# The token gather of a mixture-of-experts group, cut into four parts that each feed their own step of the gate product

## What is computed

```python
def ec_moe(h, w_r, w_gate, w_up, w_down):
    bsz, n, _ = h.shape
    cap = max(1, EC_CAPACITY * n // N_EXPERTS)          # 32 tokens per expert
    aff = jax.nn.softmax(jnp.einsum("bnd,de->bne", h, w_r).astype(jnp.float32), axis=-1)
    gates, idx = lax.top_k(jnp.swapaxes(aff, 1, 2), cap)
    bidx = jnp.broadcast_to(jnp.arange(bsz)[:, None, None], idx.shape)
    xs = h[bidx, idx]
    hid = jax.nn.silu(jnp.einsum("becd,edf->becf", xs, w_gate)) * jnp.einsum("becd,edf->becf", xs, w_up)
    ys = jnp.einsum("becf,efd->becd", hid, w_down) * gates[..., None].astype(h.dtype)
    return jnp.zeros_like(h).at[bidx, idx].add(ys)
```

## Time and profile before

| | before |
|---|---|
| runs | 1794.68, 1797.91, 1792.11 us |
| median | 1794.68 us |
| profiled execution: its own time | 1798.06 us |
| profiled execution: its span | 1796.2 us |
| mean granted TensorE clock | 0.858 of 2.4 GHz |
| PE busy | 1351.9 us (75%) |
| DVE, ACT, POOL busy | 491.3, 349.5, 152.2 us |
| HBM read | 557.69 MB, 312 GB/s over the span |

### The profile page before, as it was taken

The page is one execution under the profiler, slowest core; times in us unless marked ns, Lnnn a source line. Parts: engine busy times, 40 slices in busy tenths (PEclk is TensorE's granted clock), DMA queues, the critical chain, the costliest instruction groups (busy, mean ns, idle before and its releaser), DMA issues.

```text
span 1796.2 us, 18213 instructions
## 1 busy us (share of the span) xinstructions
PE 1351.9 (75%) x7746; PEld 786.0 (44%) x7746; DVE 491.3 (27%) x706; ACT 349.5 (19%) x515; POOL 152.2 (8%) x142
## 2 busy tenths in 40 slices
PE   3998866666685596579676665656657989899999
PEld 1653551121241141179531211212115867779997
DVE  1259440010110000056500101001005733446553
ACT  1111420000010000033200000000004632544442
POOL 1034000000000000010000000000003051440000
PEclk9999978787798898789887868779689966999999
DMA  9898839999979999994389999999999420434530
GB/s 343 354 377 349 316 132 392 422 421 422 413 299 423 412 408 423 412 357 169 148 325 421 422 422 422 422 422 422 422 422 324 170 80 33 159 137 161 186 123 24
DMA packets 109995, 561.76 MB, mean 313 GB/s; under 512 B 8516, under 2 KB 9908, under 8 KB 54126
## 3 DMA queue, kind: packets, MB, share of 16 engines
q1 hardware_dynamic: 106056, 551.83, 76.5%
q0 software_dynamic: 2208, 8.36, 1.3%
q10 hardware_dynamic: 1670, 0.68, 0.1%
HBM read 557.69 MB, written 3.16 MB: 312 GB/s over the span
## 4 chain that ended last, share of the span: by engine, by line
PE 38%; DMA 27%; DVE 3%; ACT 2%; issue 2%; SPq 0%; POOL 0%; DVEq 0%; ACTq 0%; POOLq 0%
PE ps L1838 22%; DMA ring<-in_moe_w_down 11%; DMA ring<-in_moe_w_up 11%; PE ps L2086 7%; DMA ring<-in_moe_w_gate 5%; PE ps L1823 3%; PE ps L2095 1%; PE ps L2291 1%; DMA ring<-in_w_in 1%; PE ps L2306 0%; SPq L471 0%; PE ps L2279 0%; PE ps L2119 0%; PE ps L2281 0%; ACT ring_parts L594 0%
## 5 line engine op out<-in xcount | busy, mean ns | idle before, releaser
L2086 PE MATMUL ps<-ring,scratch 128*32 128x512 f32 x3072 | 483.7, 790 | 298.3 <-DMA ring<-in_moe_w_down 126.8
L2086 PEld LDWEIGHTS ps<-ring,scratch 128*32 128x32 f32 x3072 | 130.1, 139 | 637.4 <-issue 634.6
L1838 PE MATMUL ps<-ring_parts,scratch_parts 128*128 128x512 f32 x656 | 190.6, 410 | 5.0 <-DVE xT_parts L1154 1.4
L1838 PE MATMUL ps<-scratch_parts,ring_parts 128*128 128x256 f32 x704 | 146.0, 282 | 0.0
L1838 PEld LDWEIGHTS ps<-ring_parts,scratch_parts 128*128 128x128 f32 x656 | 125.1, 193 | 38.2 <-issue 7.4
L594 ACT ACTIVATE ring_parts<-ring 128x2048 fp32r<-128x2048 f32 x56 | 106.1, 1920 | 93.7 <-PE ps L1838 87.4
L1838 PEld LDWEIGHTS ps<-scratch_parts,ring_parts 128*128 128x128 f32 x704 | 116.2, 191 | 0.3
L437 DVE TENSOR_TENSOR ring_parts<-ring,ring_parts 128x2048 fp32r<-128x2048 f32 x44 | 100.7, 2290 | 53.4 <-ACT ring_parts L594 52.1
L1438 DVE TENSOR_TENSOR scratch<-scratch,ps 128x1024 f32<-128x1024 f32 x8 | 9.8, 1221 | 300.3 <-PE ps L2086 300.3
L1446 DVE TENSOR_TENSOR scratch<-ps,gate_bc 128x512 f32<-128x512 f32 x16 | 10.3, 686 | 296.7 <-PE ps L2086 296.7
L1838 PE MATMUL ps<-xT_parts,ring_parts 128*128 128x256 f32 x288 | 80.9, 281 | 1.3 <-DVE xT_parts L1145 1.3
(11 more groups left out here) (377 smaller groups left out, 1606.2 us busy)
## 6 DMA issues: line engine op xcount, KB each, us to landing
ring<-in_moe_w_gate SPq DMA_DIRECT2D x64, 2048.0 KB, 29.0
ring<-in_moe_w_up SPq DMA_DIRECT2D x64, 2048.0 KB, 28.5
ring<-in_moe_w_down SPq DMA_DIRECT2D x64, 2048.0 KB, 32.1
ring<-in_ada_w SPq DMA_DIRECT2D x24, 2048.0 KB, 12.2
ring<-in_mlp_w SPq DMA_DIRECT2D x16, 2048.0 KB, 8.6
ring<-in_sc_w_in SPq DMA_DIRECT2D x6, 2048.0 KB, 21.3
ring<-in_w_in SPq DMA_DIRECT2D x6, 2048.0 KB, 17.8
ring<-in_xattn_wkv SPq DMA_DIRECT2D x4, 2048.0 KB, 32.3
```

The costliest lines, as they stand in the source:

```text
L1838: last = mm(out, lhs[x], rhs[y], start=start and n == 0, stop=stop and n == 2)
L2086: last = mm(ps[32 * j:32 * j + 32, banks[half], :], src[:, k, CAP * j:CAP * (j + 1)], w[j * RUN // EG][:, j % (EG // RUN), col:col + 512], ...
```

## The change

On PE, the gather is cut in four parts of two slices `k` (`gather(b)`), each into a PSUM bank of its own: 6, 7, 2 and 3 (`GATHER`). The gate product is cut in its four steps (`product_step`). The order on PE becomes: part 0, part 1, step 0, part 2, step 1, part 3, step 2, step 3. Each step waits only for the move of its own part to `xsT`: DVE moves parts 0 and 2, ACT moves parts 1 and 3. Up and down products keep their order.

```diff
@@ scalar block, experts @@
-                    act.wait_ge(sem("mo_gather"), 2 * n + 2)
-                    for k in range(4, KD):
-                        last = nc.scalar.activation(xsT[:, k, :], ps[:, 7, P * (k - 4):P * (k - 3)], ACT.Identity,
-                                                    scale=scale[:, k:k + 1], bias=shift[:, k:k + 1])
-                    last.then_inc(sem("mo_xsT_act"), 1)
+                    for b in (1, 3):
+                        act.wait_ge(sem("mo_gather"), 4 * n + (b + 1))
+                        for k in (2 * b, 2 * b + 1):
+                            last = nc.scalar.activation(xsT[:, k, :], ps[:, GATHER[b], P * (k % 2):P * (k % 2 + 1)], ACT.Identity,
+                                                        scale=scale[:, k:k + 1], bias=shift[:, k:k + 1])
+                        last.then_inc(sem("mo_xsT_act"), 1)
@@ vector block, experts: the same for b in (0, 2), with mo_xsT_dve @@
...
@@ tensor block, experts @@
-                    def product(c0, banks, src, second=None):
+                    def product_step(c0, banks, src, step):
+
+                        w = [chunk(c0 + RUN * step + q) for q in range(RUN)]
+                        for k in range(RUN * step, RUN * step + RUN):
+                            for half in range(2):
+                                for j in range(EG):
+                                    col = F * (k % RUN) + 512 * half
+                                    last = mm(ps[32 * j:32 * j + 32, banks[half], :], src[:, k, CAP * j:CAP * (j + 1)],
+                                              w[j * RUN // EG][:, j % (EG // RUN), col:col + 512],
+                                              start=(k == 0), stop=(k == KD - 1))
+                        last.then_inc(sem("chunks_used"), RUN)
...
+                    def gather(b):
+
+                        for k in (2 * b, 2 * b + 1):
+                            for t in range(NT):
+                                last = mm(ps[:, GATHER[b], P * (k % 2):P * (k % 2 + 1)], run_slice(rows[:, t, :], k),
+                                          onehot[:, t, bass.ds(g * P, P)], start=(t == 0), stop=(t == NT - 1))
+                        last.then_inc(sem("mo_gather"), 1)
 
 
                     pe.wait_ge(sem("mo_h"), 4 * n + 1)
-                    for k in range(KD):
-                        for t in range(NT):
-                            last = mm(ps[:, 6 + k // 4, P * (k % 4):P * (k % 4 + 1)], run_slice(rows[:, t, :], k),
-                                      onehot[:, t, bass.ds(g * P, P)], start=(t == 0), stop=(t == NT - 1))
-                        if k % 4 == 3:
-                            last.then_inc(sem("mo_gather"), 1)
-                    pe.wait_ge(sem("mo_xsT_dve"), n + 1)
-                    product(0, (0, 1), xsT, "mo_xsT_act")
+                    gather(0)
+                    for b in range(4):
+                        if b < 3:
+                            gather(b + 1)
+                        if b % 2:
+                            pe.wait_ge(sem("mo_xsT_act"), 2 * n + (b // 2 + 1))
+                        else:
+                            pe.wait_ge(sem("mo_xsT_dve"), 2 * n + (b // 2 + 1))
+                        product_step(0, (0, 1), xsT, b)
```

More of the change, by code:

```diff
@@ L385, in build @@
         GO = ((0, 6), (4, 7))
+        GATHER = (6, 7, 2, 3)
         MLP = [("up", 0)]
@@ L1424, in experts @@
                     n = g + GROUPS * l
[L1426 to L1430, removed]
+                    for b in (0, 2):
+                        dve.wait_ge(sem("mo_gather"), 4 * n + (b + 1))
+                        for k in (2 * b, 2 * b + 1):
+                            last = nc.vector.tensor_scalar(xsT[:, k, :], ps[:, GATHER[b], P * (k % 2):P * (k % 2 + 1)],
+                                                           scale[:, k:k + 1], shift[:, k:k + 1], ALU.mult, ALU.add)
+                        last.then_inc(sem("mo_xsT_dve"), 1)
                     dve.wait_ge(sem("mo_affbc"), n + 1)
@@ L2074, in chunk @@
                         return ring[:, slot_of(i), :].rearrange("p (e f) -> p e f", e=EG // RUN)
-                    def product(c0, banks, src, second=None):
-                        for step in range(STEPS):
[L2079 to L2089, removed]
@@ new lines, in product @@
+                    def product(c0, banks, src):
+                        for step in range(STEPS):
+                            product_step(c0, banks, src, step)
+                    def gather(b):
+                        for k in (2 * b, 2 * b + 1):
+                            for t in range(NT):
+                                last = mm(ps[:, GATHER[b], P * (k % 2):P * (k % 2 + 1)], run_slice(rows[:, t, :], k),
+                                          onehot[:, t, bass.ds(g * P, P)], start=(t == 0), stop=(t == NT - 1))
+                        last.then_inc(sem("mo_gather"), 1)
```

## The result

| | before | changed |
|---|---|---|
| runs beside each other | 20 | 20 |
| median | 1796.26 us | 1781.1 us |
| lowest to highest | 1785.82 to 1800.49 us | 1774.96 to 1796.14 us |
| ratio | | 0.9944, 95% interval 0.9926 to 0.9961 |
| profiled execution: span | 1796.2 us | 1774.6 us |

By the ratio the change is faster by 0.56%, or 10.1 us of 1796.26, where 0.41% and 7.4 us were forecast. The two medians differ by 15.2 us, the means (1795.2 and 1784.7 us) by 10.6, and the two profiled spans by 21.6. Why one change gives four such different numbers is the main question of what follows. Applied to the median on which the forecast stands, 1794.68, the ratio gives 1784.6 us, at the lower edge of the stated range (1784.4 to 1792.0); the median of 1781.1 lies under it.

What follows compares the result with a forecast made beforehand. DMA arrival of weights paces the expert stages, so the end of step 0 after each of four DMA standstills counts; 2.0 + 1.9 + 1.6 + 1.9 = 7.4 us off 1794.68 gives 1787.3 us, range 1784.4 to 1792.0.

Steps and rivals of the forecast that it cites:

- What bounds the kernel, and what leaves the path: Expert stages run at DMA pace; moving sixteen gather instructions behind step 0 saves 2.0, 1.9, 2.0, 1.9 us, before capping.
- No wait for DVE or ACT: Ahead of steps 0 and 1: moves are covered by other PE work, cost 0.0; up to 0.75 us kept for the range.
- Restart 3, 1.6 us: Expert stage start near 670 to 674 us: only a partial DMA gap to close, so the saving is capped at 1.6 us.
- The stage ends: Last down step of each stage, 5.34 or 6.59 us by the clock: each can shift up to 1.25 us, none on average.
- The sum, 7.4 us: Whole program: savings at the four expert stage starts, 2.0 + 1.9 + 1.6 + 1.9 = 7.4 us.
- the restarts: Four expert stage starts where the full DMA ring stands still until step 0 of the gate product ends; 7.4 us saved together.
- The rival of the low clock over step 0: At expert stage starts, 1.2 GHz through step 0 makes it 7.0 us; 4.6 us later in all, 1799.3 us; chance 0.05.
- restart 4: Last of the four expert stage starts, DMA at 0 GB/s at 906 to 908 us; 1.9 us saved.

Runs made afterwards that it cites:

- versions with filler: Changed kernel plus matmuls nobody reads in the first attention: five ahead of the heads, 0.9999; eleven among the first eight heads, 0.9919, both against the kernel before.
- one part ahead: Changed kernel with five unread matmuls and only one gather part ahead of each step, so each step waits openly: 1.0011 against the kernel before.

## Why the prediction was right, and where it was not

- **What bounds the kernel, and what leaves the path.** Right. The first issue came 1.6, 2.2, 1.7 and 1.8 us sooner by the gather's start, against 2.0, 1.9, 2.0 and 1.9 forecast, and the stages then took as long as before, to 0.5 us, up to the start of their last step.
- **No wait for DVE or ACT.** Right in all four traces of the change and its versions with filler: step 0 follows the gather at once, and so does step 1.
- **Restart 3, 1.6 us.** Over-sized, although the two traces that the forecast compares do differ by 1.7. The trace of before was not typical there. In five other traces with the old order the gather of restart 3 took 4.01 us at full clock and the issue came after 7.63 or 7.64 us, so the new order (7.25 to 7.28) saves 0.4 us. With the old order the clock stays up there; with the new one the stage begins where it is low, and its first sixteen instructions take 3.6 us.
- **The stage ends, "none on average".** This is the step that failed. I had the size right (5.34 to 6.59 us) and took it for chance. It is systematic. In four traces of the new order (with and without filler) 14 of the 16 last steps take 5.95 to 6.24 us; in four of the old one, besides the trace of before, all 16 take 4.93 to 5.34. About 4 of the 5.3 to 6.4 us gained at the issues are given back there. The trace of before was not typical here either, with 6.59 and 6.53 in two of its four, so that between it and the first trace of the change the last steps got shorter by 1.2 us in all.
- **The sum, 7.4 us.** The change's own effect is 4.1 and 4.8 us inside the heaps, 5.0 and 4.4 with filler, each give or take about 1 us. The 10.1 us of the comparison come from these plus the share of short runs (11 of its 20 against 2 of 20, times 13 us, about 6). So the direction was right for the reason given, the order on PE at the restarts. That 7.4 us lies in the interval is luck: the term of restart 3 was too large, the stage ends were put at nothing where they cost 4 us, and the tail was missing with its 2.2 us behind the last stage and its share of short runs. Corrected by what the runs show, it is 7.4 - 1.2 - 4 + 2.2 = 4.4 us.
- **The rival of the low clock over step 0** did not come: step 0 took 3.6 to 4.5 us. The Trainium skill's rule on cycling through PSUM banks ("TensorE: Matmul & The Clock Gate", section "A second HAM failure mode: psum-queue depth-cycling") does not show here: the bank changes left no idle time on PE at the four restarts, and the clock rose once and stayed up through the gate product. With an open wait of 1.1 us (one part ahead) step 0 took 1.9 us longer, and there too the clock rose once, only later.

**What stays open.** Why the fall and rise of the clock lie so firmly against the DMA's restart was not measured by itself. What the traces show is the distance. Where the gather began at the low clock, the first issue came 4.6 to 6.0 us after the rise with the old order (21 restarts) and 2.8 to 4.2 us after it with the new (25, without the version that is one part ahead). At the stage ends, every last step of 5.78 to 6.24 us began 1.5 to 2.5 us after a fall of the clock; those of 4.91 to 5.34 us began at most 0.8 us after one or had the fall inside them, and the two of 6.59 and 6.53 us in the trace of before began 0.8 and 1.0 us after one. A reading that fits most of this, and that no run tests by itself: the rise decides how long a restart's gather and step 0 last and so how far behind it the release comes, and the DMA then paces the stage evenly, so that the distance comes up again at its end and, after the last stage, in the tail. That the new order at restart 4 alone brings short runs supports it; the two misses above do not, nor do three more last steps with the new order: two of 5.34 us in the third stage and one of 4.91 in the fourth. What brings the clock back in the tail is open too.

## What to carry to other kernels

Where a DMA ring has run full, ask for the first release: work that can follow it should, and a part of a gather behind one step is enough. Where the DMA paces a stage, its last computation can run at either level of the clock, as the ends of 4.9 to 6.2 us show, and this can be systematic, so count it over several traces before calling it noise. And look at the heap in which the runs lie: two traces that differ by 21.6 us can hold a change worth 5, and a few filler matmuls at the one place where the clock hangs low can be worth more than the change.

## What the hardware showed that I had not expected

- The clock stayed at 0.50 for 61 us (1453 to 1514) in the trace of before, for the last 40 of them with PE busy by the profile without a gap. Most matmuls there are small, but from 1487 us on each head has three instructions of 128 rows and 512 columns, and they did not end the stretch. In the changed kernel the clock rose at 1475 us among small matmuls, with none of that size since the fall. Eleven filler matmuls of 128 rows and 512 columns among the first eight heads held it up in both kernels.
- One program has two kinds of runs 13 us apart. By the traces 10.9 of the 13 us lie in the heads of that stretch, in the same PE instructions, and 2.2 to 2.6 behind them.
- Switching PE between full-size matmuls and those of 32 output columns, four times more in each group than before, shows no gap: step 0 ends at 267.17 us and the next gather row begins at 267.10.
